# The last stage's gate product as seven quarter products and fifteen sums for each pair of token tiles

## What is computed

```python
x = x + _routed_experts(hf, eid, gate, w1[i], w3[i], w2[i]).reshape(B, S, D)
e = _rmsnorm(p[i] @ w_ple[i], g_ple_proj[i])
pg = jax.nn.sigmoid(_rmsnorm(x, g_ple[i]) @ w_ple_gate[i])
x = x + pg * e
return _rmsnorm(x, g_final)
```

## Time and profile before

| | |
|---|---|
| median of 3 runs | 2906.41 us (2905.96 to 2906.85) |
| profiled execution | 2907.55 us |
| its span, first to last instruction | 2905.6 us |
| PE busy | 2791.6 us, 96% |
| DVE busy | 1259.2 us, 43% |
| ACT busy | 860.5 us, 30% |
| mean granted TensorE clock | 0.983 of full speed |

### The profile page before, as it was taken

How to read it: one execution, slowest core, us unless ns; L and a number is a source line. 1 busy time by engine, 2 the same in 40 slices (tenths; PEclk the granted TensorE clock), 3 DMA queues, 4 the chain that set the end, 5 groups by cost and what they waited for, 6 DMA issues and landing times. The chain is left out here.

```text
span 2905.6 us, 34671 instructions
## 1 busy us (share of the span) xinstructions
PE 2791.6 (96%) x14126; PEld 1527.7 (53%) x14126; DVE 1259.2 (43%) x1816; ACT 860.5 (30%) x1315; POOL 248.4 (9%) x365
## 2 busy tenths in 40 slices
PE   8999999999999999999999979999998999999978
PEld 4676865456554767765456544434554343433334
DVE  2254536678521464436677515895232100110044
ACT  1412124466421313124566421535012000100032
POOL 0000000001120000000001220900001000000030
PEclk9999999999999999999999999999999999999989
DMA  4111110102122111110110113142319999999961
GB/s 137 32 30 37 36 26 25 56 13 102 44 80 68 25 29 45 30 37 23 58 51 23 47 65 117 42 179 77 107 59 404 423 377 411 398 397 406 423 219 72
DMA packets 141038, 379.90 MB, mean 131 GB/s; under 512 B 10448, under 2 KB 82128, under 8 KB 116176
## 3 DMA queue, kind: packets, MB, share of 16 engines
q1 hardware_dynamic: 126912, 327.34, 30.1%
q0 software_dynamic: 6912, 25.17, 2.3%
q10 hardware_dynamic: 7056, 25.17, 2.1%
HBM read 327.31 MB, written 50.33 MB: 130 GB/s over the span
## 5 line engine op out<-in xcount | busy, mean ns | idle before, releaser
L2484 PE MATMUL ex_p<-arena,ex_xT 128*32 128x512 f32 (+2 forms) x1696 | 340.9, 599 | 8.4 <-DMA arena<-in_w 7.2
L2484 PEld LDWEIGHTS ex_p<-arena,ex_xT 128*32 128x32 f32 (+2 forms) x1696 | 121.5, 133 | 210.7 <-issue 209.2
L405 PE MATMUL u_gs_b<-side,gs_w 128*128 128x512 f32 x512 | 226.3, 596 | 0.0
L405 PE MATMUL v_gs_b<-side,gs_w 128*128 128x512 f32 x512 | 226.3, 596 | 0.0
L1704 PE MATMUL mx_p<-hT,arena 128*128 128x512 f32 x512 | 220.5, 592 | 0.6 <-DMA arena<-in_w_in 0.6
L2560 DVE TENSOR_TENSOR ex_h<-ex_p,ex_s 128x512 f32<-128x512 f32 x24 | 26.8, 1119 | 359.1 <-ACT ex_s L2538 359.1
L2507 PE MATMUL ex_py<-arena,ex_hT 128*32 128x512 f32 (+2 forms) x848 | 169.5, 594 | 0.8 <-ACT ex_hT L2544 0.8
L1704 PEld LDWEIGHTS mx_p<-hT,arena 128*128 128x128 f32 x512 | 97.1, 190 | 122.3 <-issue 121.5
L405 PEld LDWEIGHTS u_gs_b<-side,gs_w 128*128 128x128 f32 x512 | 95.3, 190 | 113.5 <-issue 110.3
L405 PEld LDWEIGHTS v_gs_b<-side,gs_w 128*128 128x128 f32 x512 | 95.3, 190 | 113.5 <-issue 110.4
L401 PE MATMUL v_gs_b<-gs_w,side 128*128 128x128 f32 x1024 | 118.9, 276 | 0.0
(11 more groups left out here) (543 smaller groups left out, 4362.0 us busy)
## 6 DMA issues: line engine op xcount, KB each, us to landing
arena<-in_w SPq DMA_DIRECT2D x192, 1024.0 KB, 19.6
gs_w<-in_w_in SPq DMA_DIRECT2D x48, 512.0 KB, 4.1
slot_results<-ex_y ACTq DMA_DIRECT2D x24, 512.0 KB, 8.3
side<-in_w_out SPq DMA_DIRECT2D x8, 1024.0 KB, 11.2
x_layers<-gs_w SPq DMA_DIRECT2D x16, 512.0 KB, 2.9
arena<-x_layers SPq DMA_DIRECT2D x16, 512.0 KB, 5.6
arena<-in_w_in SPq DMA_DIRECT2D x16, 512.0 KB, 4.1
slot_results<-zero_row SPq DMA_DIRECT2D x1, 8192.0 KB, 24.1
```

Of the source, the lines that this page charges most:

```text
L405: last = nc.tensor.matmul(out[0:w, :], wt[:, n % SCAN_RING, k, 0:w], half(hT[:, k], f), start=(k == 0), stop=(k == KT - 1))
L2484: last = nc.tensor.matmul(ps[c:c + width, :], xT[:, b % 2, k, c:c + width], w13(n, j, k), start=(k == 0), stop=(k == KT - 1))
```

## The change

For two tiles a and b the product of the turned rows with the gate matrix is a 2x2 block product: rows a and b; the inner dimension in two halves of 4 parts (QK = 4); the columns in two halves of 512. It is now computed with seven block products in place of eight and with fifteen block sums (Winograd's form of Strassen's product). Four sums are of the matrix and made once (`t1` to `t4`, 128x2048 each), four are of the rows of each pair (`row_sum`, s1 to s4, 128x512 each), and seven join the products of each pair (`plus`: c11, u2, w, u3, c22, c12, c21, 128x512, each with one operand in PSUM). All are on DVE. One of the seven products, "11", is copied out of PSUM by ACT first (`kept`, 128x512).

- Each product is 4 matmuls of 128x512 into one of six PSUM banks used in turn. PSUM for turned tiles shrinks from two buffers to one. The turned tiles have four SBUF buffers in place of two.
- Scaling the matrix (`scale`, eight ACT instructions) moves from the start of `finish` to the end of `experts`, behind the issue of the last store and ahead of ACT's wait for the stores.
- The sigmoid reads SBUF in place of PSUM. Tiles a and b of a pair reach it together: a after c12, b after c21.
- The loads of x and embedding for tile t+4 and the stores of the output both are issued by SP, as store(t), load(t+4).
- For the last pair tile b alone is done in halves.

```diff
+    def scale(self, nc, act):
+        for k in range(KT):
+            if k % 4 == 0:
+                act.wait_ge(self.s_w[k // 4], 16)
+            nc.scalar.activation(self.wg[:, k], self.wg[:, k], ACT.Copy, scale=self.gain[:, k:k + 1]).then_inc(self.s_ws, 1)
...
                 act.dma_start(y_slots(N_PASS - 1), ye[:, (N_PASS - 1) % 2]).then_inc(s_o[(N_PASS - 1) % 2], 16)
+                ahead.scale(nc, act)
                 for j in range(2):
                     act.wait_ge(s_o[j], 16 * N_PASS // 2)
...
+                def store(t):
+                    sp.wait_ge(s_f, t + 1)
+                    sp.dma_start(out_dram[t * P:(t + 1) * P, :], fo[:, t % 2]).then_inc(s_o[t % 2], 16)
...
+                for t in range(TT - 1):
+                    store(t)
+                    if t + NB < TT:
+                        load(t + NB)
...
+                def product(i, n, rows, columns):
...
+                    for k in range(QK):
+                        last = nc.tensor.matmul(bank(i, n)[:], rows[:, k, :], columns[:, k, :], start=(k == 0), stop=(k == QK - 1))
+                    last.then_inc(made.sem, 1)
...
+                    product(i, "6", s2, t2)
+                    product(i, "5", s1, t1)
+                    if i < PAIRS - 1:
+                        turn(a + 2)
...
+                    product(i, "7", s3, t3)
+                    if i < PAIRS - 1:
+                        turn(b + 2)
...
+                    product(i, "3", s4, b22)
...
+                    product(i, "4", xb[:, QK:KT], t4)
...
+                for i in range(PAIRS):
+                    a, b = 2 * i, 2 * i + 1
...
+                    if i:
+                        gate_done.wait(dve, (i - 1, "a"))
+                        gated(a - 2, ALL)
+                        gate_done.wait(dve, (i - 1, "b"))
+                        gated(b - 2, ALL)
+                        dve.wait_ge(s_x5, 2 * i)
+                        out_free(a - 2)
+                        scaled(a - 2, ALL)
+                    made.wait(dve, (i, "2"))
+                    dve.wait_ge(s_kept, i + 1)
+                    plus(i, "c11", c11, v_, bank(i, "2")[:])
+                    if i:
+                        out_free(b - 2)
+                        scaled(b - 2, ALL)
+                    made.wait(dve, (i, "6"))
+                    plus(i, "u2", u_, v_, bank(i, "6")[:])
+                    if i < PAIRS - 1:
+                        front(a + 2)
+                        front(b + 2)
+                    made.wait(dve, (i, "5"))
...
+                    plus(i, "w", c12, u_, bank(i, "5")[:])
```

More of the change, by code:

```diff
@@ L2764, in _ @@
-                turn(0)
[L2765 to L2784, removed]
+                def product(i, n, rows, columns):
+                    m = products.index((i, n)) - 6
+                    if m >= 0:
+                        j, was = products[m]
+                        if was == "11":
+                            pe.wait_ge(s_kept, j + 1)
+                        else:
+                            summed.wait(pe, (j, last_reader[was]))
+                    for k in range(QK):
+                        last = nc.tensor.matmul(bank(i, n)[:], rows[:, k, :], columns[:, k, :], start=(k == 0), stop=(k == QK - 1))
+                    last.then_inc(made.sem, 1)
@@ L2798, in turned, with gate @@
                     act.wait_ge(s_t, t + 1)
[L2799 to L2806, removed]
+                    if t >= 4:
+                        made.wait(act, ((t - 4) // 2, "4"))
+                    nc.scalar.activation(xT[:, t % 4], p_t[:], ACT.Copy).then_inc(s_r, 1)
+                def gate(t, part):
+                    root_ready.wait(act, (0, t))
+                    nc.scalar.activation(sg[:, t % 2, part], sg[:, t % 2, part], ACT.Sigmoid,
+                                         scale=rs[:, 0, t:t + 1]).then_inc(s_sg, 1)
+                ALL = slice(0, D)
                 turned(0)
@@ L2810, in _ @@
                 mixed(1)
[L2811 to L2846, removed]
+                for i in range(PAIRS):
+                    a, b = 2 * i, 2 * i + 1
+                    if i:
+                        summed.wait(act, (i - 1, "c21"))
+                        gate(b - 2, ALL)
+                        act.wait_ge(s_x5, a - 1)
+                        square(xt[(a - 2) % NB], 1, a - 2)
+                    made.wait(act, (i, "11"))
+                    if i:
+                        summed.wait(act, (i - 1, "u2"))
+                    nc.scalar.activation(v_, bank(i, "11")[:], ACT.Copy).then_inc(s_kept, 1)
+                    if i:
+                        act.wait_ge(s_x5, b - 1)
+                        square(xt[(b - 2) % NB], 1, b - 2)
+                    if i < PAIRS - 1:
+                        mixed(a + 2)
+                        turned(a + 2)
+                        mixed(b + 2)
+                        turned(b + 2)
+                    summed.wait(act, (i, "c12"))
+                    gate(a, ALL)
@@ new lines, in _ @@
+                i = PAIRS - 1
+                a, b = 2 * i, 2 * i + 1
+                gate(b, slice(HALF, D))
+                summed.wait(act, (i, "c21"))
+                gate(b, slice(0, HALF))
+                act.wait_ge(s_x5, a + 1)
+                square(xt[a % NB], 1, a)
+                act.wait_ge(s_x5, a + 2)
+                act.wait_ge(s_sq, squared.order[1, a])
+                nc.scalar.activation(half(sq, 1), half(xt[b % NB], 1), ACT.Square, accum_out=extra[:]).then_inc(s_ex, 1)
@@ L2848, in _ @@
+                act.wait_ge(s_x5, a + 3)
+                nc.scalar.activation(half(sq, 0), half(xt[b % NB], 0), ACT.Square, accum_out=ss[:, 1, b:b + 1]).then_inc(s_sq, 1)
             @block.vector
@@ new lines, in _ @@
+                dve.wait_ge(s_ws, QK)
+                V.tensor_tensor(t1[:], b12, b11, ALU.subtract).then_inc(matrix_sums.sem, 1)
+                dve.wait_ge(ahead.s_rows, 16)
+                front(0)
+                dve.wait_ge(s_ws, KT)
+                matrix_sums.wait(dve, "t1")
+                V.tensor_tensor(t2[:], b22, t1[:], ALU.subtract).then_inc(matrix_sums.sem, 1)
+                front(1)
+                row_sum(0, "s1")
+                row_sum(0, "s2")
+                row_sum(0, "s3")
```

189 lines of the change are left out of this document (138 added, 51 removed).

## The result

Over 12 runs each the changed kernel takes 2910.74 us (2907.01 to 2913.65) and the kernel before 2904.82 us (2900.13 to 2908.48). The ratio is 1.0019, with a 95% interval from 1.0011 to 1.0028: slower by one to three thousandths, little but clear of no change. The time lies inside the forecast's range, 2901.5 to 2915, and the forecast, no change within 0.2% or 5.8 us, is met on the edge: the sum of its terms was +0.6 us, the measured difference of the medians is +5.9. That 2910.7 also lies inside the forecast's own 2904 to 2911 is in part luck, since the forecast was added to a median of 2906.41 from three runs, and over twelve runs the kernel before takes 1.6 us less.

The account below looks back on a forecast made before the run. The last stage was taken as start, PE's work and tail added: -13.7 + 6.1 + 2.1 + 1.2 + 1.0 + 3.9 = +0.6 us (+0.4 by the walk), so 2906.41 + 0.5 = 2907 us, no change; range 2901.5 to 2915.

Parts of the forecast that it names:

- What bounds the stage: Last stage: after the barrier, the start up to the first product, PE's own work and the tail add up.
- The products: PE, last stage: 32 of 256 records of products go, at 0.43 us each, a gain of 13.7 us.
- The scaling: ACT, before the barrier: the moved scalings delay the barrier and the gathers behind it, so the start comes 6.1 us later.
- the scaling stays hidden: Rival at the barrier: it opens where it did, 2900.8 us; chance 0.12, shared with waits that don't show.
- The sums: DVE: 0.70 us per 128x512 sum, 2.3 per 128x2048; 22.8 us for a pair against PE's 25.8.
- The dear price: Rival on DVE: sums with an operand in PSUM take 1.12 us, total 2910.4 to 2913.7 us; chance 0.08.
- the walk: The prediction's instruction-by-instruction pass through DVE's order in the last stage with assumed durations; it gave +0.4 us in total.
- nothing on the path is saved: DVE at the first gather: `t1` (2.3 us) is made while waiting, without gain, since the fourth product needs it first.
- The waits ahead of tiles 2, 4 and 6: PE waits for `front` before turning these tiles: 2.1, 1.2 and 1.0 us.
- The clock: Rival on PE: late x loads lengthen the waits and the clock falls; 7.3 us more, 2914.2 us, chance 0.2.
- The tail: From PE's last product to DVE's last instruction: 9.5 us where it was 5.6, a cost of 3.9 us.
- the clock at the start: PE's first products meet a low granted clock; the same loss as before, perhaps 1 us different either way.

Follow-up runs that it names:

- a_scale_gap: The changed kernel with the eight scalings ahead of the last store, in ACT's idle time during PE's last pass; stage 142.1 us, ratio to before 0.9990.
- a_x6: The changed kernel with six buffers for x in place of four; stage 142.7 us against the changed kernel's 148.0, ratio to before 1.0003.
- a_t1_later: The changed kernel with `t1` made behind both front sums of tiles 0 and 1, not beside the first gather; stage 145.1 us, ratio to before 1.0013.
- a_tail: The changed kernel with tile 6's multiply and add ahead of the last sum, c21, in the last pair; stage 146.1 us, ratio to before 1.0014.

## Why the prediction was right, and where its sizes were off

**What bounds the stage: right.** Start, PE's work and tail add up; seven kernels move each of them alone and together, and the stage follows.

**The products: right.** 224 records at 0.43 us, 13.7 us less. That is counted in the profile; no experiment takes products out alone.

**The scaling: right.** 6.1 us forecast for the barrier, 6.0 measured, and shown by adding it to the kernel before and by taking it away from the changed one. The rival "the scaling stays hidden" named ACT's stretch beside PE's last pass as a place where it could hide, and saw no way to it. a_scale_gap shows that it fits there, and that it takes other code than the change has.

**The sums: right in length, wrong in what lies beside them.** The 28 sums of products take 0.68 to 0.69 us and the four of the matrix 2.28 to 2.29. The dear price, 1.12, is refuted. The prediction also weighed an estimate from the Trainium skill, VectorE: DVE Perf Modes, section on the TRN2 errata, by which a sum with an operand in PSUM takes 0.07 us longer; the trace doesn't agree, with 684 ns for such sums and 685 to 692 for those with both operands in SBUF. The groups by form, after:

```profile
L2991 DVE TENSOR_TENSOR arena<-fn_kept,fn_pg 128x512 f32<-128x512 f32 x16 | 10.9, 684 | 10.0 <-PE fn_pg L2825 9.8
...
L2945 DVE TENSOR_TENSOR arena<-arena 128x512 f32<-128x512 f32 x4 | 2.8, 692 | 0.1
...
L86 POOL TENSOR_SCALAR fn_rs<-fn_ss 128x1 f32<-128x1 f32 x16 | 9.8, 613 | 86.6 <-ACT arena L2865 86.4
```

One sign of the prediction failed: DVE was to be busy near 88% between the waits. From the turn of tile 2 to that of tile 4 it was busy for 21.9 of 28.2 us, 78%, and from there to the turn of tile 6 for 22.0 of 29.7, 74%. In a_x6, where PE waits for nothing between the turns of tiles 4 and 6, it is 21.8 of 25.9 us, 84%; the walk had 22.8.

The step that failed is the sentence that `t1` would be made while DVE waits for the first gather, "nothing on the path is saved". Something was lost: beside `t1` the gather's own instruction took 2.56 us and not 0.94, on the path, 1.3 us by the first transposes, and a_t1_later takes it back. The prediction looked for what DVE's new work holds up on DVE, not on POOL.

**The waits ahead of tiles 2, 4 and 6: right in place, cause and order, off in size.** Forecast 2.1, 1.2, 1.0; measured 1.6, 2.2, 2.0. The first was taken too long because I used 0.70 for every sum, and one that waits for nothing starts every 0.60. The other two were taken too short by two terms. From the issue to its use x of tile 4 took 5.26 us, where I had 4.7 from a queue that held no store; with the 0.41 of issue that is 5.7, not 5.1. And POOL's root for tile 0 came 1.0 us late: its first instruction took 1.17 us (0.19 before) beside DVE's adds. Of these 1.6 us the sums, shorter than walked, took some 0.3 back, so the wait grew by 1.0 and by the 0.2 that stands beside it in the table. a_x6 shows that the loads are what these two waits hang on: with x there early, both are gone.

**The clock: the rival came true in part.** Its price was 7.3 us, and 3.7 of it came: 1.7 with one fall of the clock and 1.0 more in each of the two waits. I had it decide at a wait between 1.95 and 2.65 us. The clock fell behind the wait of 2.20, and cost 1.7 us, the 1.65 that the earlier trace rows gave. In the profiles of the seven experiments it fell behind waits of 2.06 (a_tail) and 2.08 (a_scale_gap) and stayed behind those of 1.6 to 2.0 us. The Trainium skill, TensorE: Matmul & The Clock Gate, section HAM oscillation — how this bites in real kernels, describes a kernel in which a wait of some 3 to 5 us between groups of matmuls throttles the engine again and again. The prediction took that over to its own, shorter waits, and by it every one of them would cost; the trace shows a fall behind one of the three, of 2.20 us. The changed kernel has one wait on each side, 2.20 and 1.99 us, so another of its executions may well lose nothing here, or twice as much. That is a guess, since one execution of each kernel was profiled, and no experiment changed the length of a wait alone. The late landing that the rival asked for, 7.1 us, came for tiles 5 and 7 (7.4 and 7.2), which PE needs 4 to 6 us later than tiles 4 and 6, and cost PE nothing.

**The tail: 3.9 forecast, 4.4 measured.** POOL's last three instructions took 0.99, 0.19 and 0.55 us where they took 0.19, 0.19 and 0.55, so 0.8 more; the first of them ran beside DVE's scaling of tile 6. DVE's queue behind the last product gave 0.2 back, 5.8 us where the walk had 6.0. a_tail shows that the queue is 1.5 us of the tail; no experiment takes POOL's 0.8 away.

**The total: on the edge, and not by mistakes that cancel.** Of the difference between forecast and measurement, 4.9 us of the stage, 1.3 is the first gather, 1.5 the waits and 0.6 what stands beside them, 1.7 the clock and 0.5 the tail, less 0.1 at the barrier and 0.6 for the clock at the start. Nearly all of it lies on the slow side. That the runs' medians differ by 5.9 and the stages by 5.5 is within the scatter.

## What to carry to other kernels

Fewer products make a stage faster only if its start and its end don't grow: here 13.7 us of PE's work bought 6.0 of barrier, 4.4 of tail and 8 of waits with the clock behind one of them, besides 1.3 for a longer gather. The barrier, the gather and the waits could be had back without touching the products, by moving instructions and with two more buffers for x; of the tail's 4.4 only 1.5. Before moving work ahead of a barrier, look which engine reaches the barrier last and whether the work fits into an idle stretch further up on its engine. And where two tiles are finished together, count the buffers again: loads that had 29 us of lead had none once a pair held all four.

## What the runs showed of the hardware

- **DVE slows POOL beside it.** Beside a 128x2048 DVE sum of two SBUF operands a gather's POOL instruction took 2.56 us, in each of the four kernels that have that sum there (changed, a_scale_gap, a_x6, a_tail), and the first gather took 0.94 in the five others. Two later gathers of the changed kernel, beside `t3` and `t4`, took 2.49 and 2.42. A 128x1 POOL instruction (L86) took 0.19 us in all 16 places before, and 1.17 beside DVE's 1024-wide adds; tile 0's next one (L87) took 0.56 us in the changed kernel and 2.69 in a_t1_later, which has a 128x2048 sum beside it. The first gather's 2.56 and the root's 2.69 are shown by an experiment, the others only by rows. The Trainium skill, SBUF — State Buffer, section Who interferes with whom, says that a VectorE instruction with two SBUF inputs contends with a GpSimd instruction that reads SBUF, and infers that tensor_tensor does not hold up the generation of a DMA's descriptors. The small instructions agree with the first. The gather is an indirect DMA that POOL generates, and it did get longer; it also reads its offsets from SBUF, and no run here tells which part of it waited.
- **A wait of PE cost more than its idle time**, by 0.2 us in each of the three. Sixteen records take 7.03 us by their own length and 6.87 where others follow at once, so 0.16 shows when nothing follows; and the eight transposes behind the wait took 1.09 to 1.10 us in place of 1.04. The second part isn't the wait's alone: in a_x6 the turns of tiles 4 and 6 took 1.09 us with no idle time ahead.
- **What a DMA's landing took depended on its place in the queue.** With the store ahead of it on the same queue, the first x of a pair landed 5.2 and 5.1 us after its issue and the second, behind another store, x and embedding, 7.4 and 7.2. With the stores on ACT's queue and one x at a time, three landed after 4.5 to 4.8 us and one after 6.2. The loads' own order in the stage changed too, so the queue's share of this stays open.
